# A dense feed-forward layer rewritten by Strassen's scheme, in a two-layer hybrid model on one core

## What is computed

```python
D_MODEL = 1024; SEQ = 256; D_FF = 2816

def swiglu(x, w1, w3, w2):
    return (jax.nn.silu(x @ w1) * (x @ w3)) @ w2

x = x + y @ w_out
x = x + swiglu(rms_norm(x, norm_ffn), ffn_w1, ffn_w3, ffn_w2)     # end of layer 0
```

## Time and profile before

| what | us |
|---|---|
| median of 3 runs (1187.43 to 1189.40) | 1188.88 |
| span of the profiled execution | 1185.6 |
| PE busy | 1136.4 |
| DVE, ACT, POOL busy | 279.9, 157.3, 52.6 |
| stretch of the dense part on PE | 182.25 to 410.6 |

### The profile page before, as it was taken

One profiled execution on the slowest core, in us unless ns is written; L12 is line 12 of the kernel. 1 busy time (PEld: TensorE's weight loads), 2 busy tenths in 40 slices (PEclk: granted clock), 3 DMA queues, 4 the chain that ended last, 5 costly groups with the idle time before them and its releaser, 6 DMA issues.

```text
span 1185.6 us, 24639 instructions
## 1 busy us (share of the span) xinstructions
PE 1136.4 (96%) x11243; PEld 786.5 (66%) x11243; DVE 279.9 (24%) x680; ACT 157.3 (13%) x340; POOL 52.6 (4%) x56
## 2 busy tenths in 40 slices
PE   7999999999999999999999999999998999999965
PEld 6889878888888888874477667776653334444321
DVE  5756544000000266442310100110101011001003
ACT  4416212000000125422000000000000000000001
POOL 0012000000000000000101001001010010000000
PEclk9999799999999999999999999999999999999999
DMA  9700095475100617687999999999999999999995
GB/s 340 299 1 2 3 362 223 142 269 191 55 1 1 273 75 286 283 343 284 391 425 423 421 425 424 425 423 423 423 424 425 426 422 426 422 425 422 425 422 204
DMA packets 65311, 358.02 MB, mean 302 GB/s; under 512 B 5396, under 2 KB 15140, under 8 KB 37296
## 3 DMA queue, kind: packets, MB, share of 16 engines
q1 hardware_dynamic: 61616, 347.26, 72.1%
q0 software_dynamic: 3136, 8.95, 2.0%
q10 hardware_dynamic: 448, 0.17, 0.1%
HBM read 350.80 MB, written 6.70 MB: 302 GB/s over the span
## 4 chain that ended last, share of the span: by engine, by line
PE 72%; SPq 17%; DMA 8%; DVE 1%; issue 1%; ACT 0%; DVEq 0%
PE ps L701 72%; SPq L531 10%; SPq L536 6%; DMA x<-in_moe 5%; DMA W<-in_moe 3%; DMA W<-in_l_w_in 0%; PE ps L763 0%; DVE W L1814 0%; DVE xn L2227 0%; PE ps L1090 0%; ACT S L1638 0%; DVE W L1840 0%; DVE S L1818 0%; ACT S L1409 0%; PE ps L1128 0%
## 5 line engine op out<-in xcount | busy, mean ns | idle before, releaser
L701 PE MATMUL ps<-W,S 128*32 128x352 f32 (+4 forms) x6216 | 506.3, 468 | 22.6 <-DMA W<-in_moe 20.3
L701 PEld LDWEIGHTS ps<-W,S 128*32 128x32 f32 (+2 forms) x6216 | 275.4, 112 | 238.8 <-issue 148.8
L701 PE MATMUL ps<-xn,W 128*128 128x256 f32 (+1 forms) x1392 | 307.3, 380 | 0.0
L701 PEld LDWEIGHTS ps<-xn,W 128*128 128x128 f32 (+1 forms) x1392 | 262.8, 189 | 39.8 <-issue 3.3
L701 PE MATMUL ps<-S,W 128*128 128x256 f32 (+2 forms) x648 | 140.4, 375 | 7.1 <-DMA W<-in_l_w_in 7.1
L2167 DVE TENSOR_TENSOR S<-S,ps 128x352 f32<-128x352 f32 x42 | 21.9, 521 | 519.0 <-ACT S L1576 516.3
L701 PEld LDWEIGHTS ps<-S,W 128*128 128x128 f32 (+2 forms) x648 | 117.1, 191 | 23.6 <-issue 8.2
L701 PE MATMUL ps<-S 128*32 128x352 f32 (+4 forms) x1488 | 126.4, 466 | 3.9 <-DMA S<-in_moe 3.8
L701 PEld LDWEIGHTS ps<-S 128*32 128x32 f32 (+1 forms) x1488 | 63.2, 113 | 56.7 <-issue 37.2
L1576 ACT ACTIVATE S<-ps 128x352 f32<-128x352 f32 x42 | 17.7, 462 | 545.2 <-PE ps L701 542.9
L1903 DVE TENSOR_TENSOR S<-S,ps 128x256 f32<-128x256 f32 x20 | 8.4, 421 | 194.6 <-ACT S L1486 194.6
(11 more groups left out here) (300 smaller groups left out, 423.0 us busy)
## 6 DMA issues: line engine op xcount, KB each, us to landing
W<-in_moe SPq DMA_DIRECT2D x116, 1408.0 KB, 32.1
W<-in_moe SPq DMA_DIRECT2D x44, 1024.0 KB, 32.1
S<-in_moe SPq DMA_DIRECT2D x33, 1024.0 KB, 32.1
W<-in_l_ffn_w SPq DMA_DIRECT2D x12, 2048.0 KB, 13.3
S<-in_moe SPq DMA_DIRECT2D x12, 1408.0 KB
x<-in_moe SPq DMA_DIRECT2D x11, 1024.0 KB
W<-in_l_ffn_w SPq DMA_DIRECT2D x6, 1536.0 KB
W<-in_l_w_in SPq DMA_DIRECT2D x4, 2048.0 KB, 19.1
```

The costliest lines, as they stand in the source:

```text
L701: return nc.tensor.matmul(o, l, r, start=start, stop=stop, **kw)
```

## The change

The 22 hidden tiles become 11 pairs (`NPAIR`) and the output's 8 tiles become 4 pairs (`ND`). The first pair is still made by `up_unscaled`, as before. For each of the other ten pairs the product of a 1024 x 256 block of `w1` (and of `w3`) with `xn` is cut in two along each of its three dimensions (hidden features, input features, tokens) and computed by seven products of quarter blocks instead of eight, in the form of Strassen's scheme with fifteen sums. A product is 4 tiles of input features for `w1` and 4 for `w3`, 8 matmuls of 128 columns. The same is done for each of the four output pairs, over all 11 pairs of hidden tiles: a product is 11 matmuls of 128 columns, and the down products now come after all up products.

The sums of the scheme are shared out. GpSimd makes four sums of weight blocks for each pair (`up_weights`, 1024 elements in each partition; `down_weights`, 1408 elements), and each waits for the one before. VectorE makes four sums of `xn` blocks once (`sx`), four sums of hidden blocks for each pair (`hidden_sums`, 128 elements each), and the sums of results out of PSUM. ScalarE copies the first product out of PSUM (`u1`). PE adds two of the products onto others in PSUM, and for this it waits for the sums that must read them first (`u2_out`, `u1_out`, `u3_out`). The weights lie in another order in DRAM, one row of 16 KB (up) or 22 KB (down) for each partition and pair, and are loaded pair by pair through three buffers (`load13`) and four (`load2`).

```diff
+            def product(q, r, first, weights, moving):
+                sides, kn = weights.shape[1], weights.shape[2]
+                for a in range(sides):
+                    for k in range(kn):
+                        ins = mm(ps[:, region(q, r), a * P:(a + 1) * P], weights[:, a, k, :], moving[:, k, :],
+                                 first and a == 0 and k == 0, k == kn - 1, skip_group_check=True)
+                ins.then_inc(prod, 1)
+
+            def up_pair(p):
...
+                product(p, 0, True, b11, xn[:, 0:4, TA])
+                pe.wait_ge(sx_done, SX0 + 2)
+                pe.wait_ge(tw_done, 4 * (p - 1) + 3)
+                product(p, 1, True, t[:, 1], sx[:, 1])
+                if p == 1:
+                    pe.wait_ge(raw_out, 2)
+                product(p, 2, True, b12, sx[:, 0])
+                pe.wait_ge(u2_out, U2 + p)
+                pe.wait_ge(sx_done, SX0 + 3)
+                product(p, 1, False, t[:, 0], sx[:, 2])
+                pe.wait_ge(tw_done, 4 * p)
...
+                product(p, 3, True, t[:, 2], xn[:, 4:8, TB])
+                pe.wait_ge(u1_out, U1 + p)
+                product(p, 0, False, b21, xn[:, 4:8, TA])
+                pe.wait_ge(u3_out, U3 + p)
+                pe.wait_ge(sx_done, SX0 + 4)
+                product(p, 2, False, b22, sx[:, 3])
...
+                pe.wait_ge(hs_done, HS0 + NPAIR)
+                pe.wait_ge(td_done, TD0 + 4 * d + 3)
+                product(q, 1, True, t[:, 1:2], hs[:, :, 5])
...
+            def up_weights(p):
+                raw, t = f13[p % 3], tw[p % 2]
+                b11, b21, b12, b22 = [raw[:, :, k:k + 4, c] for c in (TA, TB) for k in (0, 4)]
+                pool.wait_ge(in_f13[p % 3], 16 * (p // 3 + 1))
+                if p > 2:
+                    pool.wait_ge(prod, prods(p - 2, NPROD))
+                G(t[:, 0], b22, b12, ALU.subtract).then_inc(tw_done, 1)
+                pool.wait_ge(tw_done, 4 * (p - 1) + 1)
+                G(b12, b12, b11, ALU.subtract).then_inc(tw_done, 1)
+                pool.wait_ge(tw_done, 4 * (p - 1) + 2)
+                G(t[:, 1], b22, b12, ALU.subtract).then_inc(tw_done, 1)
+                pool.wait_ge(tw_done, 4 * (p - 1) + 3)
+                G(t[:, 2], b21, t[:, 1], ALU.subtract).then_inc(tw_done, 1)
...
+            for p in range(1, 4):
+                up_weights(p)
             pool.wait_ge(y_rw, 2)
-            pool.wait_ge(up_done, 6)
+            pool.wait_ge(prod, prods(2, NPROD))
             step(nc.gpsimd.memset(zero, 0.0))
...
+            for p in range(4, NPAIR):
+                up_weights(p)
+                if p == 5:
+                    down_weights(0)
+            for d in range(1, ND):
+                down_weights(d)
...
+            for p in range(1, NPAIR):
+                act.wait_ge(prod, prods(p, P1))
+                A_(u1, ps[:, region(p, 0), 0:T], ACT.Copy).then_inc(u1_out, 1)
+                act.wait_ge(prod, prods(p, P2))
+                act.wait_ge(hid_done, p)
+                A_(silp[:, 0, :], ps[:, region(p, 0), TA], ACT.Silu)
+                act.wait_ge(c_done, C0 + p)
+                A_(silp[:, 1:4, :], cs[:, 0, :, :], ACT.Silu).then_inc(silu_done, 1)
...
+            def hidden_sums(p):
+                h = [hs[:, p, i, :] for i in range(8)]
+                dve.wait_ge(hid_done, p + 1)
+                step(V.tensor_tensor(h[4], h[3], h[2], ALU.add))
+                V.tensor_tensor(h[6], h[0], h[3], ALU.subtract)
+                step(V.tensor_tensor(h[5], h[4], h[0], ALU.subtract))
+                V.tensor_tensor(h[7], h[1], h[5], ALU.subtract).then_inc(hs_done, 1)
...
+                V.tensor_tensor(u2, u1, r[1], ALU.add).then_inc(u2_out, 1)
+                dve.wait_ge(prod, prods(p, P7))
+                step(V.tensor_tensor(u3, u1, r[1], ALU.add))
+                V.tensor_tensor(both[1], pair_of(u3), pair_of(r[2]), ALU.add).then_inc(u3_out, 1)
...
+                V.tensor_tensor(both[0], pair_of(u2), pair_of(r[2]), ALU.add).then_inc(c_done, 1)
+                dve.wait_ge(silu_done, p + 2)
+                dve.wait_ge(c_done, C0 + p)
+                V.tensor_tensor(hs[:, p, 0, :], silp[:, 0, :], r[0][:, TB], ALU.mult)
+                V.tensor_tensor(hs[:, p, 1:4, :], silp[:, 1:4, :], cs[:, 1, :, :], ALU.mult).then_inc(hid_done, 1)
+                hidden_sums(p)
```

More of the change, by code:

```diff
@@ L23 @@
 RS = NF // 2
-GROUPS = [(0, 4), (4, 8), (8, 11)]
+NPAIR = NF // 2
+ND = KD // 2
+NPROD = 7
+P1, P6, P5, P7, P4, P2, P3 = range(1, NPROD + 1)
 E = 8
@@ L496, in _ @@
-            ring(f1, f3, f2, 1, lambda g: sp.wait_ge(up_done, GROUPS[g][1]),
-                 lambda g: sp.wait_ge(down_done, GROUPS[g][1]))
+            load2(0)
+            for p in range(3, NPAIR):
+                if p == 3:
+                    sp.wait_ge(up_done, 2)
+                else:
+                    sp.wait_ge(prod, prods(p - 3, NPROD))
+                load13(p)
+            sp.wait_ge(prod, prods(8, NPROD))
+            load2(1)
+            sp.wait_ge(prod, prods(9, NPROD))
@@ L996, in _ @@
             up_unscaled(1)
[L997 to L1002, removed]
+            for p in range(1, NPAIR):
+                up_pair(p)
+            for d in range(ND):
+                down_pair(d)
             def project_unscaled(i):
@@ L1481, in _ @@
                 A_(sil0[:, f, :], sil0[:, f, :], ACT.Silu).then_inc(silu_done, 1)
[L1482 to L1489, removed]
+            for p in range(1, NPAIR):
+                act.wait_ge(prod, prods(p, P1))
[5 more added lines that the diff above has]
+                A_(silp[:, 1:4, :], cs[:, 0, :, :], ACT.Silu).then_inc(silu_done, 1)
+            for d in range(ND):
+                act.wait_ge(prod, prods(NPAIR + d, P1))
+                A_(u1[:, TA], ps[:, region(NPAIR + d, 0), TA], ACT.Copy).then_inc(u1_out, 1)
+                for k in (2 * d, 2 * d + 1):
+                    act.wait_ge(res_done, 8 + k + 1)
+                    A_(sq1[:, k, :], x[:, k, :], ACT.Square).then_inc(sq_done, 1)
             norm_root(2, 5)
@@ L1894, in _ @@
                     normed(1, "l0_norm_ffn", xn)
+                    dve.wait_ge(xn_done, 2 * KD)
+                    step(V.tensor_tensor(sx[:, 0], xn[:, 0:4, TB], xn[:, 4:8, TB], ALU.add), sx_done)
+                    step(V.tensor_tensor(sx[:, 1], sx[:, 0], xn[:, 0:4, TA], ALU.subtract), sx_done)
+                    V.tensor_tensor(sx[:, 2], xn[:, 0:4, TA], xn[:, 0:4, TB], ALU.subtract).then_inc(sx_done, 1)
+                    V.tensor_tensor(sx[:, 3], xn[:, 4:8, TA], sx[:, 1], ALU.subtract).then_inc(sx_done, 1)
             for f in range(2):
@@ L1905, in _ @@
+            squares_added(6)
+            step(V.tensor_tensor(sq1[:, 0, :], sq1[:, 0, :], sq1[:, 1, :], ALU.add), sum_done)
             inverse_root(2)
```

219 lines of the change are left out of this document (145 added, 74 removed).

## The result

The changed kernel takes 1244.76 us (median of 4 runs, 1243.58 to 1245.10), the kernel before 1188.29 us beside it (4 runs, 1187.43 to 1189.40): the ratio is 1.0479, 95% interval 1.0464 to 1.0494. It is slower, as forecast, but by 56 us and not by 30: 4.8 us above the range.

The account below looks back on a forecast made before the run. The prediction took PE to bound the kernel, with every delay carried to the end. A saving of 21.4 us against waits and low clock summed to +30.4 on 1185.6, 1216.0, and with 3.3 for the median 1219 us; range 1182 to 1240.

Parts of the forecast that it names:

- PE saving: Dense part: fewer columns at 0.111 us an instruction save 13.9 us up and 7.5 down, -21.4 us together.
- stalls of pairs 2, 4, 6 to 9: Up pairs: PE waits at P7 for `u2`, 3.7 us in each of six pairs, 22.2 us.
- pair 5: Fifth up pair: it meets `down_weights(0)`, four GpSimd sums of 1408 elements, and PE stalls 5.4 us.
- first down pair: Start of the down products: P6 waits for `hidden_sums(10)` while `down_weights(1)` runs, 8.7 us.
- (a): Mixer's end: `up_weights(1)` and `(2)` run beside VectorE's last mixer step, 4 us lost, between 0 and 6.
- (b): Pair 1: `sx` follows `normed`, so `u2` comes after P5's end, 1.0 us.
- (c): Last down pair: `load2(3)` and three sums end after P6 could start, 0.9 us, between 0 and 3.
- low clock: Behind eight stalls of 2.7 us and more: half clock level costs 1.2 us each, 9.6 us.
- slip-in: Rival: up pairs' hidden sums all fit in one GpSimd gap and the saving wins, -5.7 us, 1183; chance 0.14.
- no-conflict: Rival: GpSimd and VectorE do not compete for a port at all, -18.3 us, 1171; chance 0.06.
- the case of slower weight loads: Rival: long PE rows do not keep 0.111 us; at 0.132 1204 us without any stall, more with them; chance 0.08.
- that rival: Rival: GpSimd becomes the bound, strided blocks at over 2.3 us a sum, 1240 us or more; chance 0.10.

Follow-up runs that it names:

- e4_filled_stalls: Changed kernel with 18 extra matmuls that nothing reads between P5 and P7 of the seven stalled pairs; 1236.96 us, ratio 1.0421 to the kernel before.
- e2_sums_later: Changed kernel with VectorE's hidden sums of pair p - 1 made behind `u3_out` of pair p; 1194.95 us, ratio 1.008 to the kernel before.
- e8_half_sums: Changed kernel with each GpSimd sum of the up pairs cut into two of 512 elements; 1218.67 us, ratio 1.0264 to the kernel before.
- e3_mixer_first: Changed kernel with GpSimd's `up_weights(1)` after the second `y_rw` and `up_weights(2)` after `sum_done`; 1238.73 us, ratio 1.0426 to the kernel before.
- e5_down_later: Changed kernel with GpSimd starting `down_weights(1)` only when `hidden_sums(10)` are done; 1234.00 us, ratio 1.0397 to the kernel before.
- e6_all_reordered: Changed kernel with hidden sums behind `u3_out`, mixer before GpSimd's first sums, `down_weights(0)` after the last up pair's sums, `down_weights(1)` after the last hidden sum; 1178.28 and 1179.32 us.

## Why the prediction was too small

The mechanism was right: VectorE's operations in SBUF wait for whole GpSimd sums, PE waits for `u2`, in the pairs named and no others, and the saving on PE is lost several times over. The sum was 26.4 us too small (30.4 against 56.8), by its terms:

| term | predicted | measured | how measured |
|---|---|---|---|
| PE saving | -21.4 | -20.4 | 12.50 and 68.7 us |
| stalls of pairs 2, 4, 6 to 9 | 22.2 | 30.5 | their idle times |
| pair 5 | 5.4 | 7.1 | idle time |
| first down pair | 8.7 | 10.8 | 1.54 + 9.24 |
| (a) mixer's end | 4.0 | 6.2 | idle time |
| (b) pair 1 | 1.0 | 0 | 12.50 us |
| (c) last down pair | 0.9 | 0.9 | idle time |
| low clock | 9.6 | 23.2 | left over beside the idle times: 17.2 up, 2.4 down, 3.6 before |
| carried to the end | 0 | -1.5 | 773.5 against 775.0 |

**The clock is the step that failed most, 13.6 of the 26.4 us.** "I take 1.2 each, 9.6 us, between 0 and 1.7 each" came from one stall of 2.7 us, with 3.4 us at half level. In the seven stalled pairs slow work cost 1.6 to 3.2 us each, and at the stalls of 5.3 us in pairs 6 to 9 the low level lasted 6.8 us. With the first down pair the eight stalls counted came to 19.6 us against 9.6, 10.0 of the 13.6. The other 3.6 stand at the mixer's end, whose wait of 6.2 us the prediction had in two halves of 2 us each and gave no price of the clock. The bound was drawn from the one row there was, though it was a row about a shorter stall. `e4_filled_stalls` shows that the time belongs to the clock: with PE kept busy, the same late `u2` costs 12.9 us less. What decides between 3.4 and 6.8 us of low level, or none (pair 10 in the two profiles above), is open.

**The stall per pair is the second, 8.3 us.** The prediction had the right ladder with one operation per gap (4.8 us), and then took the middle towards two. The ground was that GpSimd needs 0.31 us behind its own semaphore, from a row with a transfer behind it. It needs 0.08, and one slips in; pair 7's timeline shows it, and only `h5` shares a gap. Where GpSimd has no semaphore between two instructions, `h5` got none either (`e2_sums_later`, `e8_half_sums`). The gap being uncertain on one side, the end and not the middle was the value to take. The sum itself measured 2.34 to 2.37 us, not 2.0: the estimate of 2.25 from the Trainium skill ("GPSIMD Engine Reference", section "3.1 Elementwise — side-by-side cycle accounting") was nearer than the earlier trace rows, where one of the two operands is broadcast. One operation per gap at 2.43 us a step gives the 5.3 us seen; `e8_half_sums` shows that the step is what counts.

**(a), the mixer's end,** counted three operations in each half. DVE's two TENSOR_SCALAR operations have one tensor in SBUF and were left out, but waited too: 4.75 us for both, 0.73 without GpSimd beside them. `e3_mixer_first` took this idle time away and gave 6.0 us net.

**Pair 5 and the first down pair** were sized with 2.75 us for a sum of 1408; it takes 3.16. At the first down pair the chain ended 13.6 us behind the last up product (386.08 to 399.71), past the 9.8 to 12.5 of the prediction. `e5_down_later` gave back 10.8 us in the medians.

**What held.** 0.111 us for an instruction of 128 columns (0.1116 over rows of hundreds); pairs 3 and 10 undisturbed; transfers hidden; and everything behind the dense part moved one to one but for 1.5 us, the transfers there at 0.98 of their time against 0.97. The 0.9 us at the last down pair came out to the tenth by luck: the terms written down give 10.3 + 3 x 2.75 = 18.6 us against 19.6 and need 1.9 us of gaps for a wait of 0.9. In the trace the transfer took 10.3 us and the three sums 10.0, with gaps of 0.08. (b) did not come: pair 1 lost nothing.

**The rivals.** The slip-in and no-conflict cases are excluded by pair 7's timeline, and the case of slower weight loads by 0.1116 us in rows of 462 instructions. GpSimd never was the bound: its four sums take 10 us of a pair (312.76 to 322.71), and no wait of PE in the up pairs ended at `tw_done`. The time of that rival, 1240 or more, came about by another way. Of the versions built, those with all four changes of order reach 1176 to 1179 us, so the scheme gains up to 1.05% here when DVE's operations in SBUF are kept away from what PE waits for.

## What to carry to other kernels

Work given to GpSimd is not free because GpSimd is idle: each of its SBUF instructions can hold up one VectorE operation in SBUF for its whole length, so count how many such operations stand ahead of the result that TensorE waits for, and price each at a whole GpSimd instruction. Order VectorE's list so that only operations that are needed at once stand there, follow what the moved ones now hold up, or make GpSimd's instructions shorter. Where a wait of several microseconds is forecast on TensorE, add the slow clock behind it from a row with a stall as long, and where there is none, leave the bound open upward. Give it a range even then, since the same stall was followed by slow work in one profile and by none in another.

## What the runs showed of the hardware

- GpSimd starts a sum 0.08 us behind its own semaphore. A plain sum of 1024 elements takes 2.34 to 2.37 us, of 1408 3.16, of 512 1.27; with a broadcast operand it was 1.90 and 2.00.
- VectorE's TENSOR_SCALAR with one tensor in SBUF waited for GpSimd too (2.4 us each against 0.37), an operation with an operand in PSUM did not (0.42 in both cases).
- The granted clock was at the 1.2 GHz level for 6.8 us around the end of four stalls of 5.3 us and for 3.4 us around that of a fifth. Of four stalls of 2.10 us in `e8_half_sums` two were followed by slow work and two were not; a stall of 2.7 us was in one profile of `e6_all_reordered` and not in another; idle times of 1.3 us in `e4_filled_stalls` and 2.2 us in `e3_mixer_first` were not.
